# VectorE reads a finished projection step before it splits the next weights, in sixteen steps of a hybrid decoder layer

## The chip, the cores and the metric

The kernel runs on one core of one Trainium2 chip. The metric is the device time of one execution in microseconds (us); several executions of a kernel are compared by their median.

## The reference

One inference step of a one-layer decoder trunk over 320 tokens (256 of a prompt and 8 x 8 new ones), in float32. All token vectors go through one large input projection; two branches are then computed from its parts, merged and projected out. Cut to what matters here:

```python
def layer(x, p, s0, g_pre, w_in, g_v, w_s, b_s, w_a2, b_a, g_o, w_pa, w_pb, w_o, g_post, w_pg, w_pe):
    xn = rms_norm(x, g_pre)
    u_a, v_a, z_a, q_b, k_b, v_b, z_b, a_lr, m_a, m_b = split_cols(xn @ w_in)
    v_a = rms_norm(v_a, g_v)
    y_a = chunk_spatial_gate(u_a, v_a, w_s, b_s) * jax.nn.silu(z_a)
    log_a = jax.nn.log_sigmoid((a_lr @ w_a2 + b_a).astype(jnp.float32)) / GATE_TAU
    ...
    o, s_new = gla(q, k, v, log_a.reshape(B, L, HB, DK), s0)
    y_b = rms_norm(o, g_o).reshape(B, L, E_B) * jax.nn.silu(z_b)
    m = jax.nn.sigmoid(m_a) * (y_a @ w_pa) + jax.nn.sigmoid(m_b) * (y_b @ w_pb)
    h = x + rms_norm(m @ w_o, g_post)
    h = h + jax.nn.sigmoid(h @ w_pg) * (p @ w_pe)
    return h, s_new, v_a
```

The change touches the columns `v_b` (1024 wide: the values of the gated linear attention `gla`) and `z_b` (1024 wide: the gate of its output).

## The kernel before

**Steps and units.** Every projection is cut into steps of 128 output features. A step is a product of 16 blocks of 128 x 128 weights with all 320 tokens and ends up in one PSUM bank; its weights come as two units of 8 blocks (512 KB each). The order of the steps is fixed by the constants S_K, S_Q, S_V, S_ZB, S_VA, S_ZA, S_U, S_GATE and so on: four k steps, four q steps, eight v steps (s = S_V + t), eight z steps (s = S_ZB + t), eight va steps and further ones. In the v and z steps a step's bank is `bank[s % 2]`.

**Split products.** To keep float32 accuracy each unit is split into a rounded part and a rest: ScalarE writes `w_hi` = rounded(`w_raw`) (`split_hi`, L416), VectorE writes `w_lo` = `w_raw` - `w_hi` (`low`, L739, called twice by `split_lo`, and called "a rest" below). TensorE multiplies hi x hi, hi x lo and lo x hi (`product`, L1382 to L1384), 24 matmuls a unit and 48 a step.

**The ring.** `w_raw`, `w_hi` and `w_lo` have four slots, so units run two steps ahead: in step s, ScalarE and VectorE split the units of step s + 2. Half 0 of `split_lo(s)` waits until TensorE has used the first unit of step s, half 1 until it has used the second one, which is the end of step s. SP issues the load of unit u as soon as the rest of unit u - 4 is written (semaphore lo_ready, L377 and L338).

**Who reads a bank.** When step s has ended (`sums(s)` waits for it) VectorE scales the bank by the tokens' norm. In the v steps it writes `v_b` (L948 before); in the z steps `gate_input` (L964) writes `tmp`, which waits in addition for the gate of two steps before. Both count up acc_read. TensorE starts step s only when step s - 2 has been read (same bank). ScalarE's `sigmoid(s)` (L481) waits for the read of step s and stands behind both halves of its `split_hi(s)`; GpSimd's `gate` (L1291) multiplies the two.

**What else VectorE does in these steps.** After read and rests come, in v step 0, `spans` (L815 to L818), then `gla_inputs` (decay products of q and k), and in v step 4 to z step 7 transposes of 32 x 32 blocks that turn v and k into token rows (`v_to_tokens` L934, `k_to_tokens` L970). In z step 0 it masks the attention blocks (L985, L991). The transposes of z step 6 complete `v_tokens`. ScalarE rounds them in z step 7 (`round_v(1)`, L493), GpSimd writes their rests in two instructions (`split_v`, L1299; semaphore vp_lo), and TensorE's eight `o_and_state` products behind z step 7 (L1486 to L1488) need them: product 4 the first of the two, product 6 the second, product 7 also the read of z step 7. In the last step of this stretch:

```python
                if t == 7:
                    pe.wait_ge(ak_split, 6)
                    pe.wait_ge(acc_read, S_VA - 1)
                    for i in range(KE):
                        if i in (0, 4, 6):
                            pe.wait_ge(vp_lo, {0: 1, 4: 2, 6: 3}[i])
                        if i == KE - 1:
                            pe.wait_ge(acc_read, S_VA)
                        o_and_state(i)
```

Every engine works through its instructions in the order in which they are written; nothing else orders them but semaphores.

Of the kernel before, what the change touches and what calls it, by code (L numbers as in the profile page):

```python
# [101 lines left out]
def build(nc, A, O):  # L102
    ctx = ExitStack()
    with ctx:
# [618 lines left out]
        def _(dve):  # L723
# [12 lines left out]
            def low(q, ready, used):  # L736
                dve.wait_ge(hi_ready, ready)
                dve.wait_ge(units_used, used)
                dve.tensor_tensor(wlo[:, q], raw[:, q], whi[:, q].bitcast(F32), ALU.subtract).then_inc(lo_ready, 1)  # L739

            def split_lo(s, i=None, halves=(0, 1)):

                for half in halves:
                    u = 2 * (s + 2) + half
                    low(2 * (s % 2) + half, *((u + 1, u - 3) if i is None else (4 * i + (u + 1), 4 * i + (u - 3))))

            def sums(s, i=None, by=4):

                dve.wait_ge(units_used, 2 * s + 2 if i is None else by * i + (2 * s + 2))
# [58 lines left out]
            def spans():  # L808

                prompt = [x[:, :, 0:SEQ].rearrange("p h (c t) -> p h c t", t=BLK) for x in (cum, q_mid, k_dec)]  # L810
                dec = [x[:, :, SEQ:T].rearrange("p h (c t) -> p h c t", t=DEC_L) for x in (cum, k_dec)]
                mid = prompt[0][:, :, :, MID:MID + 1].to_broadcast([P, HB, NBLK, BLK])
                end = prompt[0][:, :, :, BLK - 1:BLK].to_broadcast([P, HB, NBLK, BLK])
                end_d = dec[0][:, :, :, DEC_L - 1:DEC_L].to_broadcast([P, HB, DEC_B, DEC_L])
                dve.tensor_tensor(prompt[1], prompt[0], mid, ALU.subtract).then_inc(spans_ready, 1)  # L815
                dve.tensor_copy(q_mid[:, :, SEQ:T], cum[:, :, SEQ:T]).then_inc(spans_ready, 1)
                dve.tensor_tensor(prompt[2], end, prompt[0], ALU.subtract).then_inc(spans_ready, 1)
                dve.tensor_tensor(dec[1], end_d, dec[0], ALU.subtract).then_inc(spans_ready, 1)  # L818
# [97 lines left out]
            def k_dec_to_tokens(n):  # L916

                ct, pf = n // 4, n % 4
                rows, to = slice(BLK * ct, BLK * ct + BLK), slice(BLK * pf, BLK * pf + BLK)
                dve.transpose(k_ts[rows, :].rearrange("p (h f) -> p h f", f=DK)[:, :, to],  # L920
                              k_dec[to, :, SEQ + BLK * ct:SEQ + BLK * ct + BLK]).then_inc(kts_ready, 1)

            def v_dec_to_tokens(n):

                ct, pf = n // 4, n % 4
                rows, to = slice(BLK * ct, BLK * ct + BLK), slice(BLK * pf, BLK * pf + BLK)
                dve.transpose(v_ts[rows, :].rearrange("p (i f) -> p i f", f=P)[:, :, to],
                              v_sb[to, :, SEQ + BLK * ct:SEQ + BLK * ct + BLK]).then_inc(vts_ready, 1)
# [9 lines left out]
            def some_v_to_tokens(s):  # L938
                if s in VT_STEPS:
                    first, n = VT_STEPS[s]  # L940
                    dve.wait_ge(acc_read, S_V + 4 if first + n <= 16 else S_V + KE)
                    for m in range(first, first + n):
                        v_to_tokens(m)

            for t, s in enumerate(range(S_V, S_ZB)):
                split_lo(s)
                sums(s)
                acc_t.up(dve.tensor_tensor(v_sb[:, t, :], bank[s % 2][:, 0:T], r, ALU.mult))  # L948
                if t == 0:
                    spans()  # L950
                else:
                    gla_inputs(t - 1)
                if t >= 6:
                    dve.wait_ge(dve_own, own.value)
                    for n in range(4 * (t - 6), 4 * (t - 6) + 4):
                        k_dec_to_tokens(n)
                some_v_to_tokens(s)

            def gate_input(s, n):

                sums(s)
                if n >= 2:
                    dve.wait_ge(gate_ready, n - 1)
                acc_t.up(dve.tensor_tensor(tmp[:, s % 2, :], bank[s % 2][:, 0:T], r, ALU.mult))  # L964

            def k_to_tokens(n):

                ct, pf = n // 4, n % 4
                rows, to = slice(BLK * ct, BLK * ct + BLK), slice(BLK * pf, BLK * pf + BLK)
                dve.transpose(ak[rows, :, :, SEQ:SEQ + DK].rearrange("p c h f -> p h c f")[:, :, :, to],  # L970
                              k_256[to, :, :].rearrange("p h (c q t) -> p h c q t", c=2, t=BLK)[:, :, :, ct, :])\
                   .then_inc(kdt_ready, 1)

            for t, s in enumerate(range(S_ZB, S_VA)):
                split_lo(s)
                gate_input(s, t)
                if t == 0:

                    dve.wait_ge(att_zeroed, 4)
                    dve.wait_ge(att_done, 1)  # L980
                    for c in range(2):
                        for g in range(4):
                            b0, b1 = BLK * g, BLK * g + BLK
                            mask = con[b0:b1, C_ATT + b0:C_ATT + b1].bitcast(I32).unsqueeze(1).to_broadcast([BLK, HB, BLK])
                            last = dve.copy_predicated(ak[b0:b1, c, :, P * c + b0:P * c + b1], mask,  # L985
                                                       bank[4][b0:b1, P * c:P * c + P]
                                                       .rearrange("p (h t) -> p h t", h=HB))
                        last.then_inc(att_masked, 1)
                    for h in range(HB):
                        r0 = DEC * (h % 2)  # L990
                        last = dve.copy_predicated(att_s[:, h, :], con[r0:r0 + DEC, C_ATS:C_ATS + DEC].bitcast(I32),  # L991
                                                   bank[3][r0:r0 + DEC, DEC * (h // 2):DEC * (h // 2) + DEC])
                    last.then_inc(att_masked, 1)
                if t == 1:
                    dve.wait_ge(acc_read, S_V + KE)
                    for n in range(2 * (P // BLK)):
                        v_dec_to_tokens(n)
                some_v_to_tokens(s)
                if s in KT_STEPS:
                    first, n = KT_STEPS[s]  # L1000
                    dve.wait_ge(gla_in, 6)
                    for m in range(first, first + n):
                        k_to_tokens(m)
# [763 lines left out]
```

## Time and profile before

| | us |
|---|---|
| median of 3 executions | 952.49 (952.32 to 952.87) |
| the profiled execution | 952.29 |
| its span, first to last instruction | 950.3 |
| TensorE (PE) busy | 945.9 (100%) |
| VectorE (DVE) busy | 569.3 (60%) |
| ScalarE (ACT) busy | 377.3 (40%) |
| GpSimd (POOL) busy | 122.9 (13%) |

The profile's page gives busy time by engine, the chain of work that ended last, and groups of instructions. The trace behind it gives every instruction with its start and duration. A matmul of 320 columns is shown with 0.31 us, but matmuls are pipelined and start 0.147 us apart (24 of them make 3.52 us, a unit; 48 make 7.04 us, a step), so a short pause of TensorE doesn't show as idle time and has to be read from the distance between starts. The granted TensorE clock is at full speed in all 40 slices of the page. The v steps run from about 66 to 122.4 us, the z steps from there to 181.5 us (with 2.1 us of attention matmuls behind the first), and the `o_and_state` products to 188.6 us.

### The profile page before, as it was taken

How to read it: one execution, taken by the hardware profiler on the slowest of the kernel's cores; microseconds unless marked ns; L12 is line 12 of the kernel's file. 1: busy time of each engine (PE TensorE's matmuls, PEld its weight loads, DVE VectorE, ACT ScalarE, POOL GpSimd, SP SyncE). 2: the span in 40 equal slices, each digit the busy share in tenths (PEclk: the TensorE clock that was granted, in tenths of full speed). 3: DMA queues.
4: the chain of work that ended last, by engine and by line, in shares of the span. 5: the costliest groups of instructions: out<-in, count | busy, mean ns of one | idle time of the engine just before them, and what ended most of it. 6: DMA issues, size and time to landing. Idle time of an engine off the chain costs nothing.

```text
span 950.3 us, 17375 instructions
## 1 busy us (share of the span) xinstructions
PE 945.9 (100%) x6632; PEld 939.0 (99%) x6632; DVE 569.3 (60%) x800; ACT 377.3 (40%) x484; POOL 122.9 (13%) x113
## 2 busy tenths in 40 slices
PE   9999999999999999999999999999999999999998
PEld 9999999999999999999999999999999999999998
DVE  6948779737889866444444444444445444597442
ACT  7545245522353444333333333333333233555331
POOL 1000005504212740000000000000002433100000
PEclk9999999999999999999999999999999999999999
DMA  9545436977654544444444444444447444336541
GB/s 349 181 131 182 142 128 196 229 253 256 221 157 155 186 141 154 154 154 145 144 153 154 135 154 153 154 141 146 154 155 268 145 154 154 111 134 227 176 157 37
DMA packets 56671, 159.69 MB, mean 168 GB/s; under 512 B 6452, under 2 KB 20280, under 8 KB 56632
## 3 DMA queue, kind: packets, MB, share of 16 engines
q1 hardware_dynamic: 42496, 143.05, 45.8%
q10 hardware_dynamic: 14136, 16.10, 5.1%
q8 instruction: 27, 0.44, 0.2%
q14 instruction: 12, 0.10, 0.0%
HBM read 149.94 MB, written 9.18 MB: 167 GB/s over the span
## 4 chain that ended last, share of the span: by engine, by line
PE 100%; DVE 0%; issue 0%; POOL 0%; DVEq 0%; POOLq 0%
PE bank L1382 30%; PE bank L1384 30%; PE bank L1383 30%; PE bank L1443 1%; PE bank L1452 1%; PE bank L1642 1%; PE bank L1636 1%; PE bank L1446 1%; PE bank L1639 1%; PE bank L1415 0%; PE bank L1413 0%; PE bank L1414 0%; PE bank L1420 0%; PE bank L1546 0%; PE bank L1585 0%; PE bank L1486 0%
## 5 line engine op out<-in xcount | busy, mean ns | idle before, releaser
L739 DVE TENSOR_TENSOR w_lo<-w_raw,w_hi 128x1024 fp32r<-128x1024 f32 x252 | 314.4, 1253 | 319.8 <-ACT w_hi L633 165.9
L1382 PE MATMUL bank<-x_hi,w_hi 128*128 128x320 f32 x1216 | 376.6, 310 | 0.0
L1384 PE MATMUL bank<-x_hi,w_lo 128*128 128x320 f32 x1216 | 375.7, 309 | 0.0
L1383 PE MATMUL bank<-x_lo,w_hi 128*128 128x320 f32 x1216 | 375.7, 309 | 0.0
L416 ACT ACTIVATE w_hi<-w_raw 128x1024 fp32r<-128x1024 f32 x148 | 156.0, 1058 | 252.8 <-PE bank L1384 234.9
L1382 PEld LDWEIGHTS bank<-x_hi,w_hi 128*128 128x128 f32 x1216 | 228.2, 188 | 2.0 <-issue 1.8
L1383 PEld LDWEIGHTS bank<-x_lo,w_hi 128*128 128x128 f32 x1216 | 228.2, 188 | 0.0
L1384 PEld LDWEIGHTS bank<-x_hi,w_lo 128*128 128x128 f32 x1216 | 228.2, 188 | 0.0
L633 ACT ACTIVATE w_hi<-w_raw 128x1024 fp32r<-128x1024 f32 x96 | 101.7, 1059 | 115.7 <-PE bank L1384 115.7
L1382 PE MATMUL bank<-m_hi,w_hi 128*128 128x320 f32 x448 | 138.4, 309 | 0.0
L1383 PE MATMUL bank<-m_lo,w_hi 128*128 128x320 f32 x448 | 138.4, 309 | 0.0
L1384 PE MATMUL bank<-m_hi,w_lo 128*128 128x320 f32 x448 | 138.4, 309 | 0.0
L1382 PEld LDWEIGHTS bank<-m_hi,w_hi 128*128 128x128 f32 x448 | 84.1, 188 | 0.0
L1383 PEld LDWEIGHTS bank<-m_lo,w_hi 128*128 128x128 f32 x448 | 84.1, 188 | 0.0
L1384 PEld LDWEIGHTS bank<-m_hi,w_lo 128*128 128x128 f32 x448 | 84.1, 188 | 0.0
L1364 POOL TENSOR_TENSOR sig<-mo 128x320 f32<-128x320 f32 x1 | 1.6, 1632 | 376.0 <-DVE mo L1185 376.0
L1382 PE MATMUL bank<-ya_hi,w_hi 128*128 128x320 f32 x128 | 39.6, 309 | 0.0
L1383 PE MATMUL bank<-ya_lo,w_hi 128*128 128x320 f32 x128 | 39.6, 309 | 0.0
L1384 PE MATMUL bank<-ya_hi,w_lo 128*128 128x320 f32 x128 | 39.6, 309 | 0.0
L1382 PE MATMUL bank<-yb_hi,w_hi 128*128 128x320 f32 x128 | 39.6, 309 | 0.0
L1383 PE MATMUL bank<-yb_lo,w_hi 128*128 128x320 f32 x128 | 39.6, 309 | 0.0
L1384 PE MATMUL bank<-yb_hi,w_lo 128*128 128x320 f32 x128 | 39.6, 309 | 0.0
(250 smaller groups left out, 924.3 us busy)
## 6 DMA issues: line engine op xcount, KB each, us to landing
w_raw<-in_w_units SPq DMA_DIRECT2D x258, 512.0 KB, 3.3
state_dec<-in_s ACTq DMA_DIRECT2D x8, 512.0 KB, 6.4
out_st_dec<-state_dec ACTq DMA_DIRECT2D x8, 512.0 KB, 5.7
h<-in_x_t ACTq DMA_DIRECT2D x4, 640.0 KB, 8.3
out_y<-pe_out ACTq DMA_DIRECT2D x16, 160.0 KB, 2.5
x_sb<-in_x_t SPq DMA_DIRECT2D x6, 320.0 KB, 7.6
v_rows<-v_parts SPq DMA_DIRECT2D x4, 256.0 KB
v_stacked_rows<-v_rows SPq DMA_DIRECT2D x4, 256.0 KB, 6.4
```

The lines of the kernel that those rows point to most:

```text
L416: act.activation(whi[:, q], raw[:, q], ACT.Copy).then_inc(hi_ready, 1)
L633: act.activation(whi[:, q], raw[:, q], ACT.Copy).then_inc(hi_ready, 1)
L739: dve.tensor_tensor(wlo[:, q], raw[:, q], whi[:, q].bitcast(F32), ALU.subtract).then_inc(lo_ready, 1)
L1382: pe.matmul(acc, h, hi[:, k0 + k, :], start=first and k == 0, stop=False)
L1383: pe.matmul(acc, h, lo[:, k0 + k, :], start=False, stop=False)
L1384: m = pe.matmul(acc, l, hi[:, k0 + k, :], start=False, stop=last and k == UK - 1)
L1443: pe.matmul(bank[n][:, 0:T], whi[:, c % 4, w, :], xhi[:, k, :], start=k == 0, stop=False)
L1446: pe.matmul(bank[n][:, 0:T], whi[:, c % 4, w, :], xlo[:, k, :], start=False, stop=False)
L1452: m = pe.matmul(bank[n][:, 0:T], wlo[:, c % 4, w, :], xhi[:, k, :], start=False, stop=k == KX - 1)
L1636: pe.matmul(bank[PG_BANKS[n]][:, 0:T], whi[:, c % 4, w[n], :], mhi[:, k, :], start=k == 0, stop=False)
L1639: pe.matmul(bank[PG_BANKS[n]][:, 0:T], whi[:, c % 4, w[n], :], mlo[:, k, :], start=False, stop=False)
L1642: m = pe.matmul(bank[PG_BANKS[n]][:, 0:T], wlo[:, c % 4, w[n], :], mhi[:, k, :], start=False, stop=k == KX - 1)
```

## The change

In the eight v steps the read of the finished step (`sums(s)` and the product with `r`) now stands ahead of both rests of `split_lo(s)`; in the eight z steps `gate_input(s, t)` stands ahead of them. Nothing is added or removed, and only VectorE's order changes.

```diff
@@ -943,9 +943,9 @@
             for t, s in enumerate(range(S_V, S_ZB)):
-                split_lo(s)
                 sums(s)
                 acc_t.up(dve.tensor_tensor(v_sb[:, t, :], bank[s % 2][:, 0:T], r, ALU.mult))
+                split_lo(s)
                 if t == 0:
                     spans()
                 else:
@@ -972,8 +972,8 @@
             for t, s in enumerate(range(S_ZB, S_VA)):
+                gate_input(s, t)
                 split_lo(s)
-                gate_input(s, t)
                 if t == 0:
```

VectorE at the first two v steps; `v_b` is written by the read, `w_lo` by the rests, `decay_cum` by the last work of the q steps, and q_mid and k_dec by `spans`:

```order
 L857 SCALAR_TENSOR_TENSOR decay_cum<-consts,k_dec 128x320 x4
-L739 TENSOR_TENSOR w_lo<-w_raw,w_hi 128x1024 x2
-L948 TENSOR_TENSOR v_b<-bank,r_tok 128x320
+L947 TENSOR_TENSOR v_b<-bank,r_tok 128x320
+L739 TENSOR_TENSOR w_lo<-w_raw,w_hi 128x1024 x2
 L815 TENSOR_TENSOR q_mid<-decay_cum 128x4x256
 L816 COPY q_mid<-decay_cum 128x4x64
 L817 TENSOR_TENSOR k_dec<-decay_cum 128x4x256
 L818 TENSOR_TENSOR k_dec<-decay_cum 128x4x64
```

The read has moved ahead of two rests; what follows stands where it stood.

VectorE at the fifth to seventh z step (t = 4 to 6); `tmp` is written by the read, `att_and_kd` and `v_tokens` by the transposes:

```order
-L739 TENSOR_TENSOR w_lo<-w_raw,w_hi 128x1024 x2
-L964 TENSOR_TENSOR tmp<-bank,r_tok 128x320
+L964 TENSOR_TENSOR tmp<-bank,r_tok 128x320
+L739 TENSOR_TENSOR w_lo<-w_raw,w_hi 128x1024 x2
 L970 STREAM_TRANSPOSE att_and_kd<-k_67 32x4x2x32 x8
-L739 TENSOR_TENSOR w_lo<-w_raw,w_hi 128x1024 x2
-L964 TENSOR_TENSOR tmp<-bank,r_tok 128x320
+L964 TENSOR_TENSOR tmp<-bank,r_tok 128x320
+L739 TENSOR_TENSOR w_lo<-w_raw,w_hi 128x1024 x2
 L934 STREAM_TRANSPOSE v_tokens<-v_b 32x4x2x32 x8
```

Between the transposes of one step and the rests of the next there now stands a wait for the end of that next step; before, only the second of the two rests waited for it.

## Rows read from the trace of the kernel before

**Rows 1.** page, part 1, whole run: engine, busy us (share of the span) xinstructions
```profile
PE 945.9 (100%) x6632; PEld 939.0 (99%) x6632; DVE 569.3 (60%) x800; ACT 377.3 (40%) x484; POOL 122.9 (13%) x113
```

**Rows 2.** page, part 4, the chain that ended last, share by engine
```profile
PE 100%; DVE 0%; issue 0%; POOL 0%; DVEq 0%; POOLq 0%
```

**Rows 3.** all waits of PE: engine line <- releaser: us, times, longest
```profile
PE bank L1420 <- POOL att_and_kd L1270: 1.1, 1, 1.1
```

**Rows 4.** timeline of PE, 79.7 to 80.4: start us, us, instruction
```profile
79.75 0.31 PE L1384 MATMUL bank<-x_hi,w_lo 128*128 128x320 f32 x1
79.97 0.41 PE L1382 MATMUL bank<-x_hi,w_hi 128*128 128x320 f32 x1
80.21 0.30 PE L1383 MATMUL bank<-x_lo,w_hi 128*128 128x320 f32 x1
80.36 0.31 PE L1384 MATMUL bank<-x_hi,w_lo 128*128 128x320 f32 x1
```

**Rows 5.** timeline of DVE, end of the q steps and first v steps
```profile
77.07 2.36 DVE L739 TENSOR_TENSOR w_lo<-w_raw,w_hi 128x1024 fp32r<-128x1024 f32 x2
79.35 0.48 DVE L948 TENSOR_TENSOR v_b<-bank,r_tok 128x320 f32<-128x320 f32 x1
79.75 1.21 DVE L815 TENSOR_TENSOR q_mid<-decay_cum 128x1024 f32<-128x1024 f32 x1
```

**Rows 6.** timeline of ACT, v steps and z steps six to eight
```profile
94.40 1.06 ACT L416 ACTIVATE w_hi<-w_raw 128x1024 fp32r<-128x1024 f32 x1 [2.45 <-PE bank L1384]
...
104.96 1.06 ACT L416 ACTIVATE w_hi<-w_raw 128x1024 fp32r<-128x1024 f32 x1 [2.46 <-PE bank L1384]
...
167.70 1.06 ACT L416 ACTIVATE w_hi<-w_raw 128x1024 fp32r<-128x1024 f32 x1 [2.46 <-PE bank L1384]
170.45 0.47 ACT L481 ACTIVATE sig<-tmp 128x320 f32<-128x320 f32 x1 [1.69 <-DVE tmp L964]
...
174.74 1.06 ACT L416 ACTIVATE w_hi<-w_raw 128x1024 fp32r<-128x1024 f32 x1 [0.78 <-PE bank L1384]
...
181.88 1.06 ACT L493 ACTIVATE v_tokens_hi<-v_tokens 128x1024 fp32r<-128x1024 f32 x1 [2.33 <-DVE v_tokens L934]
```

**Rows 7.** timeline of DVE, fourth v step and z steps five to eight
```profile
92.26 1.23 DVE L739 TENSOR_TENSOR w_lo<-w_raw,w_hi 128x1024 fp32r<-128x1024 f32 x1
...
163.54 3.72 DVE L970 STREAM_TRANSPOSE att_and_kd<-k 32x256 f32<-32x256 f32 x8
...
174.05 1.40 DVE L739 TENSOR_TENSOR w_lo<-w_raw,w_hi 128x1024 fp32r<-128x1024 f32 x1
175.83 1.86 DVE L739 TENSOR_TENSOR w_lo<-w_raw,w_hi 128x1024 fp32r<-128x1024 f32 x1 [0.39 <-ACT w_hi L416]
...
178.12 3.72 DVE L934 STREAM_TRANSPOSE v_tokens<-v_b 32x256 f32<-32x256 f32 x8
...
183.92 1.48 DVE L739 TENSOR_TENSOR w_lo<-w_raw,w_hi 128x1024 fp32r<-128x1024 f32 x1 [0.82 <-ACT w_hi L416]
```

**Rows 8.** loads of w_raw issued from 73 to 130, us to landing
```profile
DMA to landing us min/median/max: 3.1/3.3/4.8
```

**Rows 9.** the same of all weight loads
```profile
DMA to landing us min/median/max: 3.0/3.3/10.5
```

**Rows 10.** timeline of POOL at the seventh and eighth z step
```profile
174.32 4.66 POOL L1306 TENSOR_TENSOR att_and_kd_lo<-att_and_kd,att_and_kd_hi 128x512 fp32r<-128x512 f32 x3
...
183.02 3.54 POOL L1299 TENSOR_TENSOR v_tokens_lo<-v_tokens,v_tokens_hi 128x512 fp32r<-128x512 f32 x2 [3.20 <-ACT v_tokens_hi L493]
```

**Rows 11.** the first of the two instructions of the last row alone
```profile
183.02 1.29 POOL L1299 TENSOR_TENSOR v_tokens_lo<-v_tokens,v_tokens_hi 128x512 fp32r<-128x512 f32 x1 [3.20 <-ACT v_tokens_hi L493]
```

**Rows 12.** timeline of PE, seventh o_and_state product and its neighbour
```profile
186.71 0.28 PE L1488 MATMUL bank<-att_and_kd_hi,v_tokens_lo 128*128 128x256 f32 x1
186.83 0.34 PE L1486 MATMUL bank<-att_and_kd_hi,v_tokens_hi 128*128 128x384 f32 x1
```

## The prediction

> **What bounds the kernel now.** I read the page's busy times first, then the chain of waits, then TensorE's own waits, and only then the timelines of the sixteen steps. TensorE is busy for 945.9 of 950.3 us [rows 1] and the chain that ended last is TensorE at 100% [rows 2]. In the whole run it has one wait that the trace lists, 1.1 us before its very first matmuls [rows 3], far from the v and z steps. VectorE is busy for 60% [rows 1]. So what VectorE does earlier or later counts only where TensorE waits for it. The question is then not how much earlier the bank is read, but which instruction of TensorE stood behind that read before, and which one stands behind something that is now later.
>
> TensorE's pauses are hidden by pipelined durations, so I looked at distances between starts. In the v and z steps 320-column matmuls start 0.147 us apart (80.21 to 80.36 is 0.15). There is one exception that concerns this change: at the border between v steps 1 and 2 the starts are 79.75, 79.97, 80.21 [rows 4]. Two distances take 0.46 us in place of 2 x 0.147 = 0.29, so 0.17 us are lost. The third v step needs the bank of the first, and VectorE read that bank from 79.35 for 0.48 us, to 79.83 [rows 5]; TensorE goes on 0.14 us later. The read was late because VectorE was late from its work on the decays: it came free at 77.07 and then did two rests, 2.28 us from start to the read's start [rows 5].
>
> **What the change does, part by part.**
>
> The eight v reads. The only one TensorE waited for is the first. It now starts at 77.07, as its step ended a step's length before the pause, at about 72.9, and nothing else holds it, and ends at 77.55, 2.3 us before TensorE asks. That pause goes: minus 0.17 us. The two rests behind it end 0.40 us later (79.35 less 0.08 of overlap in place of 79.75 is where the next work begins [rows 5]), at about 78.7 and 79.8. TensorE needs the first at 79.9, so 1.2 us of cover remain, and the second 3.5 us later. `spans` starts where it did, at 79.75, since the same three instructions stand ahead of it. What would be late next is the first rest; it would have to lose 1.2 us.
>
> The other reads, seven v and eight z. A read may be as late as the end of the following step, 7.04 us after its own, so moving it from 2.3 us behind the end to the end itself brings nothing: 0 us.
>
> What follows the rests. The decay products of v step 7, which TensorE needs 7.04 us after that step's end, and the masks of z step 0 start at most 0.5 us later (2.7 us behind the end where it was 2.3; in z step 0 VectorE waits for 2.1 us of attention matmuls anyway). Nothing that TensorE waits for within a step hangs on them. Cost 0 us.
>
> The rests. In a v step without a backlog the first rest ran in mid-step: in v step 3 from 92.26 to 93.49 [rows 7], where the step ended when ScalarE began its second half at 94.40 [rows 6]. Now it must wait for that end and the read: 94.40 + 0.40 + 1.23 = 96.0, 2.5 us later. TensorE uses it at the end of the next step, 101.4; 5.4 us of cover. The second rest waited for ScalarE (1.06 us) and ran to 94.40 + 2.3; now to 94.40 + 0.40 + 2.4 = 97.2, against a use at 104.9. Cost 0 us.
>
> The loads behind the rests. SP issues a load when a rest is written, so one of two loads is also up to 2.5 us later. The one that follows the rest of v step 3 would go out at 96.0. The longest landing between 73 and 130 us is 4.8 us [rows 8], so 100.8, and ScalarE rounds this unit at 104.96 [rows 6]: 4.1 us of cover. With the longest landing of the whole run, 10.5 us [rows 9], it would be 106.5. ScalarE would be 1.6 us late, but VectorE asks for the result only at 108.5 + 0.4, and TensorE at 115.5. In the z steps VectorE was already late for its first rest (its transposes ended at 163.54 + 3.72 = 167.26, the step at 167.70 [rows 6, 7]), so loads move by only 1 us there. Cost 0 us.
>
> The sigmoid and the gate. `sigmoid` waited for the read: in z step 5 it ran at 170.45, though ScalarE was free at 167.70 + 1.06 = 168.76 [rows 6]. It now goes at once, and GpSimd's gate and what follows it come up to 1.7 us earlier. No product waits for a gate here, but this moves GpSimd's long instructions against VectorE's rests, which matters next.
>
> The transposes and what hangs on them. After the step's end there came, before, 1.09 us of waiting for ScalarE, one rest and the read: the transposes of z step 4 began at 163.54, 2.9 us after the end at 160.66 (167.70 less a step). Now come the read and two rests: 0.40 + 2.28 = 2.7 us, more if the rests are stretched. In z step 6 the distance was 178.12 - 174.74 = 3.38 us, as the rests took 1.40 and 1.86 us while GpSimd worked from 174.32 on, in place of 1.23 [rows 6, 7, 10]. The new distance lies between 2.7 us (no rest is stretched) and 2.7 + 2 x 0.63 + 0.15 = 4.1 us (both like the worse one), that is from 0.7 earlier to 0.7 later. Since GpSimd's block moves ahead by up to 1.7 us, I take 0.3 us earlier.
>
> From here a chain with very little cover leads to TensorE. The transposes end at 181.84; ScalarE rounds from 181.88 [rows 6]; GpSimd writes two rests from 183.02 to 186.56 [rows 10], the first 1.29 us [rows 11], the second 2.24, stretched by 0.95, while VectorE's rest ran from 183.92, itself 1.48 us instead of 1.23 [rows 7]. The seventh product starts at 186.83 [rows 12], 0.27 us after GpSimd's end; 0.14 us of this is what a released TensorE needed above. The true cover is 0.13 us, and since TensorE comes 0.17 us earlier, it is due by 186.66. The new order: transposes end about 181.5, GpSimd starts at about 182.7, takes again 3.54 us, and ends at 186.2, with 0.3 us to spare. But VectorE's two rests now lie at about 182.0 and 183.7, so both can meet GpSimd's two instructions. Bounds: no stall, if the pair meets one rest as before, and 0.7 + 0.95 - 0.13 + 0.17 = 1.7 us, if the transposes are late by the full 0.7 and the first instruction is stretched as the second was. I take 0, as the nearest row is this pair with one meeting.
>
> The rows show the collision as a stretch: 1.86 for 1.23, 2.24 for 1.29. The Trainium skill, on its page "SBUF — State Buffer", section "Who interferes with whom", has a harsher rule: a VectorE instruction with two SBUF inputs contends with a GpSimd instruction that reads SBUF through a port held exclusively, so that the one that comes second is blocked until the other has ended. By this rule the two engines would take turns at z step 7, which is rival B.
>
> Sum in the profiled execution's own time: 952.29 - 0.17 + 0 = 952.12 us. The three runs shown have a median of 952.49, 0.2 us above the profiled one, so I forecast 952.3 us as a median. That is 0.02% less, and this kernel's measurement can't tell less than about 0.2% (1.9 us) from no change.
>
> **Rivals.**
>
> B. VectorE and GpSimd take turns. Place: the pair of GpSimd rests ahead of product 6. GpSimd wants to begin at 182.7, waits for VectorE's rest until 183.2, ends at 184.5; VectorE's second rest waits for that and ends at 185.7; GpSimd's second instruction only then runs, to 187.0. With 0.14 us TensorE goes on at 187.1, not at 186.66: a stall of about 0.5 us, net plus 0.3, thus 952.8. The bound of 1.7 us gives 954.0. It decides from the point where the pair takes more than 3.9 us in place of 3.54. For it: this is the only place in the two stages where TensorE's cover is a tenth of a microsecond. Against it: GpSimd's earlier block leaves VectorE freer in z step 6, so the chain may start earlier.
>
> C. The later loads starve the ring. Place: w_raw's slots in the v and z steps. It decides when a load takes more than 115.5 - 96.0 - 1.06 - 1.23 = 17 us. Price: each microsecond above this is a microsecond of TensorE in each of up to sixteen steps, so one more in all would be 968. Against it: the longest of all landings is 10.5 us [rows 9].
>
> D. A gain above 0.2%. It needs 1.9 us of TensorE's pauses in the two stages. For it: the read frees a bank 2.3 us earlier in most steps. Against it: the starts show 0.17 us of pause that this can remove. Time 950.4, if there were pauses that the records hide.
>
> E. The change does not do what it says, because VectorE arrives late at most steps. In the z steps it was free only 0.4 us ahead of the step's end (167.26 against 167.70), so stretched instructions could push the read back behind the end again. Time as in the forecast or, if also the first v read is still late, 952.5.
>
> **Chances.** Forecast, hidden but for the 0.17 us: 0.70, with its own range of 952.0 to 952.8 (the spread of the runs shown is 0.55 us). B: 0.23. C: 0.02. D: 0.02. E: 0.03. Together, range 951.9 to 953.4: it takes in all of the forecast and E and most of B. Faster by over 0.2%: 0.02 (D). Slower by over 0.2%: 0.03, from C and the far end of B. Within 0.2%: 0.95.
>
> **What would show it.** The starts around 79.9 us are 0.15 apart, with the v read of step 0 near 77.1. The z reads start within 0.2 us of ScalarE's second half, and the sigmoids directly behind it. The rests in v steps lie as a pair behind the read. The list of TensorE's waits stays as short as it is. For B, a distance between starts well above 0.18 us ahead of the seventh `o_and_state` product, and a pair of L1299 that takes over 3.9 us. I am wrong if the time leaves 952.3 by more than 1.9 us, or if TensorE pauses at any other border of the two stages.

## The result: slower by 0.36%, outside the forecast range

| | kernel before | changed kernel |
|---|---|---|
| median, us (7 runs each) | 952.53 (951.91 to 952.92) | 956.35 (954.53 to 956.51) |
| the profiled execution, us | 952.29 | 955.05 |
| its span, us | 950.3 | 953.2 |

The ratio is 1.0036, with a 95% interval of 1.0026 to 1.0046. The forecast was 952.3 us, with a range of 951.9 to 953.4.

The seven runs of the changed kernel form two groups: 954.53 and 955.05 us with a mean granted clock of 1.000, and five from 956.33 to 956.51 us with 0.998 (the granted clock is the share of TensorE's full speed that the chip let it run at, here as the mean of a run). The profiled execution, 955.05 us, is of the first group. So there are two things to explain: 2.9 us of span, and 1.3 to 1.5 us on top of that in most runs.

The page of the changed kernel, parts 1 and 4, answers to [rows 1, 2]:

```profile
PE 946.4 (99%) x6632; PEld 939.4 (99%) x6632; DVE 572.5 (60%) x800; ACT 377.3 (40%) x484; POOL 126.2 (13%) x113
...
PE 96%; DVE 3%; issue 1%; POOL 0%; ACT 0%; DVEq 0%; POOLq 0%
```

TensorE's work is the same, but it no longer makes up the whole chain; VectorE holds 3% of it. All waits of TensorE, to be held against [rows 3]:

```profile
PE bank L1486 <- POOL v_tokens_lo L1299: 2.4, 2, 2.2
PE bank L1420 <- POOL att_and_kd L1270: 1.1, 1, 1.1
```

There is a new wait, 2.4 us in two pieces, for GpSimd's rests of `v_tokens`. The timeline of TensorE there (with the products counted from 0, 184.91 is the last matmul of product 3, 187.38 the first of product 4, 189.61 the first of product 6):

```profile
184.91 0.28 PE L1488 MATMUL bank<-att_and_kd_hi,v_tokens_lo 128*128 128x256 f32 x1
187.38 0.44 PE L1486 MATMUL bank<-att_and_kd_hi,v_tokens_hi 128*128 128x384 f32 x1 [2.19 <-POOL v_tokens_lo L1299]
187.66 0.34 PE L1487 MATMUL bank<-att_and_kd_lo,v_tokens_hi 128*128 128x384 f32 x1
...
189.14 0.28 PE L1488 MATMUL bank<-att_and_kd_hi,v_tokens_lo 128*128 128x256 f32 x1
189.61 0.45 PE L1486 MATMUL bank<-att_and_kd_hi,v_tokens_hi 128*128 128x384 f32 x1 [0.19 <-POOL v_tokens_lo L1299]
```

Neighbouring starts are 0.12 us apart at such places. 187.38 - 184.91 - 0.12 is 2.35 us, 189.61 - 189.14 - 0.12 is 0.35 us, and the first matmul behind each pause is followed after 0.28 to 0.29 us where 0.18 is usual. Together 2.9 us, the whole difference of the spans. (Product 6 stood at 186.83 before [rows 12].) The next step then begins at 191.49 in place of 188.60, and nothing behind it gives anything back.

Where GpSimd got late is seen by going back: ScalarE's rounding (L493), then GpSimd's pair of rests.

```profile
184.58 1.06 ACT L493 ACTIVATE v_tokens_hi<-v_tokens 128x1024 fp32r<-128x1024 f32 x1 [5.20 <-DVE v_tokens L934]
```

In [rows 6] ScalarE began this at 181.88. It is 2.7 us late because VectorE's transposes ended 2.7 us late. The timeline of VectorE from z step 3 to z step 6 (L964 is the read, L739 the two rests, L970 and L934 the transposes):

```profile
153.54 0.49 DVE L964 TENSOR_TENSOR tmp<-bank,r_tok 128x320 f32<-128x320 f32 x1 [0.53 <-PE bank L1384]
153.94 5.52 DVE L739 TENSOR_TENSOR w_lo<-w_raw,w_hi 128x1024 fp32r<-128x1024 f32 x2
159.39 3.69 DVE L970 STREAM_TRANSPOSE att_and_kd<-k 32x256 f32<-32x256 f32 x8
163.11 0.49 DVE L964 TENSOR_TENSOR tmp<-bank,r_tok 128x320 f32<-128x320 f32 x1
163.51 3.04 DVE L739 TENSOR_TENSOR w_lo<-w_raw,w_hi 128x1024 fp32r<-128x1024 f32 x2
...
170.34 0.49 DVE L964 TENSOR_TENSOR tmp<-bank,r_tok 128x320 f32<-128x320 f32 x1
170.75 3.04 DVE L739 TENSOR_TENSOR w_lo<-w_raw,w_hi 128x1024 fp32r<-128x1024 f32 x2
...
177.43 0.49 DVE L964 TENSOR_TENSOR tmp<-bank,r_tok 128x320 f32<-128x320 f32 x1
177.84 2.96 DVE L739 TENSOR_TENSOR w_lo<-w_raw,w_hi 128x1024 fp32r<-128x1024 f32 x2
180.82 3.72 DVE L934 STREAM_TRANSPOSE v_tokens<-v_b 32x256 f32<-32x256 f32 x8
```

The read of z step 3 is on time, then its pair of rests takes 5.52 us. Alone two rests take 2.35. The first of the two by itself:

```profile
153.94 3.28 DVE L739 TENSOR_TENSOR w_lo<-w_raw,w_hi 128x1024 fp32r<-128x1024 f32 x1
```

And GpSimd over the same time:

```profile
149.96 3.81 POOL L1306 TENSOR_TENSOR att_and_kd_lo<-att_and_kd,att_and_kd_hi 128x1024 fp32r<-128x1024 f32 x3
153.73 2.41 POOL L1322 TENSOR_TENSOR v_parts<-v_tokens_dec,v_parts 64x1024 fp32r<-64x1024 f32 x1
156.10 2.28 POOL L1322 TENSOR_TENSOR k_parts<-k_tokens_dec,k_parts 64x512 fp32r<-64x512 f32 x1
...
164.18 1.29 POOL L1291 TENSOR_TENSOR zb_gate<-tmp,sig 128x320 f32<-128x320 f32 x1 [3.98 <-ACT sig L481]
...
185.72 3.84 POOL L1299 TENSOR_TENSOR v_tokens_lo<-v_tokens,v_tokens_hi 128x512 fp32r<-128x512 f32 x2 [4.18 <-ACT v_tokens_hi L493]
```

GpSimd began the 2.41 us instruction that reads v_tokens_dec (L1322) at 153.73, 0.21 us ahead of VectorE's rest. The rest takes 3.28 us and ends 1.08 us behind the end of GpSimd's instruction, which is about its own length. GpSimd's next one (1.28 us when alone) then takes 2.28. They did not share time, they took turns. In the kernel before, the same place looked like this on GpSimd:

```profile
150.72 5.88 POOL L1306 TENSOR_TENSOR att_and_kd_lo<-att_and_kd,att_and_kd_hi 128x1024 fp32r<-128x1024 f32 x3
156.56 2.40 POOL L1322 TENSOR_TENSOR v_parts<-v_tokens_dec,v_parts 64x1024 fp32r<-64x1024 f32 x1
```

There v_parts ran from 156.56, when VectorE was at its transposes, which do not slow it (2.40 us).

From z step 4 on the lag of 2.5 us is not worked off. From read to read VectorE needs 7.23, 7.09 and 7.15 us (163.11, 170.34, 177.43, 184.58), and TensorE 7.04. The late pairs of rests take 2.96 to 3.04 us, since a GpSimd instruction gets in between the two: in z steps 4 and 5 it is the gate, at 164.18 and 171.41, in z step 6 the last part of the split of the attention block (L1306), which began at 177.98 and took 1.73 us.

### The profile page after: what moved, and what is told of

Same layout as the page of the kernel before. It is cut to its first block, busy times and chain, and to the rows that moved or that the text cites. A ratio compares the mean times of both kernels' runs of the same rounds, so it can differ in the third digit from the quotient of the medians.

```text
span 953.2 us, 17379 instructions
## 1 busy us (share of the span) xinstructions
PE 946.4 (99%) x6632; PEld 939.4 (99%) x6632; DVE 572.5 (60%) x800; ACT 377.3 (40%) x484; POOL 126.2 (13%) x113
## 4 chain that ended last, share of the span: by engine, by line
PE 96%; DVE 3%; issue 1%; POOL 0%; ACT 0%; DVEq 0%; POOLq 0%
PE bank L1382 29%; PE bank L1384 29%; PE bank L1383 29%; DVE w_lo L739 2%; PE bank L1443 1%; PE bank L1636 1%; PE bank L1452 1%; PE bank L1446 1%; PE bank L1642 1%; PE bank L1639 1%; PE bank L1414 0%; PE bank L1415 0%; PE bank L1413 0%; DVE v_tokens L934 0%; DVE att_and_kd L970 0%
## 5 line engine op out<-in xcount | busy, mean ns | idle before, releaser
L739 DVE TENSOR_TENSOR w_lo<-w_raw,w_hi 128x1024 fp32r<-128x1024 f32 x252 | 317.6, 1270 | 303.2 <-ACT w_hi L633 165.9
```

## The experiments

All were timed beside the kernel before (27 runs of it in each of two batches, medians 952.55 and 952.49 us).

**V steps alone.**

```diff
             for t, s in enumerate(range(S_V, S_ZB)):
-                split_lo(s)
                 sums(s)
                 acc_t.up(dve.tensor_tensor(v_sb[:, t, :], bank[s % 2][:, 0:T], r, ALU.mult))
+                split_lo(s)
```

> The kernel before with the new order in the eight v steps alone; the z steps keep the old one. Theory 1 (all of the loss comes from the z steps, where VectorE's rests meet GpSimd's instructions; GpSimd does nothing in the v steps): 952.3 us, the pause of 0.17 us at 79.9 us gone, rests in z step 3 at 1.2 to 1.3 us each, no wait of TensorE for v_tokens_lo. Theory 2 (the later rests and loads of the v steps carry a part of the loss): over 953.3 us.

Measured 951.99 us, ratio 0.9996 (0.9987 to 1.0005); no wait of TensorE but the one before its first matmuls; the pause near 79.9 us is gone, and the rests of z step 3 take 1.23 and 1.28 us. The loss is not in the v steps. This is also the lowest median of all kernels here, but it can't be told from no change.

**Z steps alone.**

```diff
             for t, s in enumerate(range(S_ZB, S_VA)):
-                split_lo(s)
                 gate_input(s, t)
+                split_lo(s)
```

> The kernel before with the new order in the eight z steps alone. Theory 1: the whole loss, 956.5 us as a median, a first rest of z step 3 of about 3.3 us and a wait of TensorE of some 2.2 us ahead of the fifth o_and_state product; the runs fall into two groups, near 955 with a granted clock of 1.000 and near 956.5 with 0.998, as those of the changed kernel. Theory 2: clearly less than that, under 955.5.

Measured 956.52 us, ratio 1.0039 (1.0026 to 1.0053), the pair of rests in z step 3 again 5.52 us, and TensorE's longest wait 2.2 us. Two runs lie at 955.28 and 955.41 us (clock 1.000), three from 956.52 to 956.83 (0.998). The z steps carry the whole loss.

**The changed kernel with the old order in z step 3, and the kernel before with the new order in z step 3 alone.**

```diff
             for t, s in enumerate(range(S_ZB, S_VA)):
+                if t == 3:
+                    split_lo(s)
                 gate_input(s, t)
-                split_lo(s)
+                if t != 3:
+                    split_lo(s)
```

(and the reverse: `t != 3` ahead, `t == 3` behind.)

> The changed kernel with the old order in z step 3 alone. There a rest of 3.28 us had begun 0.2 us behind a GpSimd instruction that reads v_tokens_dec. Theory 1a (this one meeting makes the lag, the later steps only keep it): no rest over 1.9 us in z step 3, the transposes of z step 6 start within 0.5 us of 178.1, TensorE stalls 0 to 0.6 us at the o_and_state products, 952.3 to 953.0 us. Theory 1b (each z step loses by the gate that GpSimd now runs during the rests, 3.0 us for the pair in place of 2.3, so the lag builds up anyway): transposes of z step 6 over 1.5 us late, 954.5 us or more.

> The kernel before with the new order in z step 3 alone. GpSimd's split of the attention block starts only at 150.7 us as before, since the sigmoid of z step 2 is not earlier, so the meeting of z step 3 may fall on another of its instructions. Theory 1a: the pair of rests in z step 3 takes 2.4 to 4.5 us; a lag of up to 2 us is worked off by 0.6 us a step in the three steps behind it, as the old order meets no gate in the rests; 952.5 to 953.5 us. Theory 1b: the same place alone costs nothing: 952.5 us.

Old order in z step 3: 954.32 us, ratio 1.0018 (1.0009 to 1.0027). Theory 1a failed in its numbers: going back to the old order there did not keep the rests free. Nor did theory 1b get a clean hit: the transposes of z step 6 started at 179.72, 1.6 us late, and the pairs of rests of z steps 4 and 5 took 3.0 us, as it said, but the time stayed below its 954.5. This run doesn't decide between the two. VectorE, two rests and the read:

```profile
152.87 5.13 DVE L739 TENSOR_TENSOR w_lo<-w_raw,w_hi 128x1024 fp32r<-128x1024 f32 x2
157.92 0.47 DVE L964 TENSOR_TENSOR tmp<-bank,r_tok 128x320 f32<-128x320 f32 x1
```

GpSimd's first reading instruction of L1322 (L1325 in this kernel):

```profile
153.53 3.38 POOL L1325 TENSOR_TENSOR v_parts<-v_tokens_dec,v_parts 64x1024 fp32r<-64x1024 f32 x1
```

The sigmoids and gates of the steps ahead were still early, so v_parts started near 153.5 instead of 156.6. This time VectorE's first rest was there ahead of v_parts (152.87; it took 1.79 us itself, as the last part of GpSimd's L1309 had begun 0.03 us before it), GpSimd waited for it (3.38 us in place of 2.41), and VectorE's second rest waited for GpSimd.

New order in z step 3 alone: 953.79 us, ratio 1.0015 (1.0006 to 1.0024). Theory 1b (952.5 us) falls; theory 1a was right in kind but its bounds were too small, 4.5 us for the pair and 953.5 us for the time. VectorE, read and rests of z step 3, and the transposes of z step 6:

```profile
153.95 0.49 DVE L964 TENSOR_TENSOR tmp<-bank,r_tok 128x320 f32<-128x320 f32 x1 [0.51 <-PE bank L1387]
154.35 5.00 DVE L739 TENSOR_TENSOR w_lo<-w_raw,w_hi 128x1024 fp32r<-128x1024 f32 x2
...
180.01 0.90 DVE L934 STREAM_TRANSPOSE v_tokens<-v_b 32x256 f32<-32x256 f32 x2
```

GpSimd (L1309 and L1325 are L1306 and L1322 of the kernel before):

```profile
151.11 3.81 POOL L1309 TENSOR_TENSOR att_and_kd_lo<-att_and_kd,att_and_kd_hi 128x1024 fp32r<-128x1024 f32 x3
154.89 3.39 POOL L1325 TENSOR_TENSOR v_parts<-v_tokens_dec,v_parts 64x1024 fp32r<-64x1024 f32 x1
```

Here nothing of GpSimd's was early. But the wait for the step's end leaves VectorE idle from about 153.4 to 153.95; GpSimd's two short instructions of the attention split are no longer held up by rests (3.81 us for the three, 5.88 before), and v_parts comes at 154.89, behind the start of the pair, which takes 5.0 us. So both parts of the new order lead to the same meeting: the earlier sigmoid and the later first rest. The lag shrinks behind it, as no gate runs between the rests of z steps 4 and 5 (2.36 us a pair): the transposes of z step 6 start at 180.01, 1.6 us later than in the kernel with the v steps alone.

**GpSimd writes the parts, but reads nothing for them.**

```diff
                     for n, (parts, x) in enumerate(((v_parts, v_ts), (k_parts, k_ts))):
                         pool.wait_ge(parts_hi, n + 1)
-                        pool.tensor_tensor(parts[:, 1, :], x[:], parts[:, 0, :].bitcast(F32), ALU.subtract)\
-                            .then_inc(parts_lo, 1)
+                        pool.memset(parts[:, 1, :].bitcast(F32), 0.0).then_inc(parts_lo, 1)
```

> The changed kernel, but GpSimd fills the rests of v_parts and k_parts (L1322) with zeros and reads nothing for them; so the lower parts of the new tokens' v and k are left out of the computation. Theory 1a, corrected by the two runs on z step 3 (the rests of z step 3 are held up by whatever long reading instruction GpSimd has under way, and the lag is kept since each later pair of rests meets a gate): the pair of rests in z step 3 takes 2.3 to 3.0 us, the transposes of z step 6 start at about 178.1 instead of 180.8, TensorE stalls under 0.6 us, 952.3 to 953.0 us. Rival 3 (the instructions compete in some other way, by their number or their writes): the pair still takes over 4 us and the time stays over 954.5.

Measured 952.73 us, ratio 1.0001 (0.9992 to 1.0010). The pair of rests in z step 3 on VectorE, and the two fills on GpSimd at the same moment:

```profile
154.19 2.35 DVE L739 TENSOR_TENSOR w_lo<-w_raw,w_hi 128x1024 fp32r<-128x1024 f32 x2
```

```profile
153.95 0.95 POOL L1322 MEMSET v_parts<- 64x1024 f32 x1
154.84 0.52 POOL L1322 MEMSET k_parts<- 64x512 f32 x1
```

With fills of 0.95 and 0.52 us right beside it the pair takes 2.35 us, its length alone. The loss is gone. The transposes of z step 6 start at 178.48, and TensorE waits for nothing there. (The fills are also shorter than the instructions that they replace, so the time alone would not tell reading from length. But the first fill runs from 153.95 to 154.90, and the first rest, which starts at 154.19, isn't stretched. Whether a fill is longer beside a rest than alone was not measured.)

**The same work one gate later.**

```diff
                 if t == 2:
                     split_att_and_kd(0, 0, SEQ)
+                if t == 3:
                     for n, (parts, x) in enumerate(((v_parts, v_ts), (k_parts, k_ts))):
```

> The changed kernel, but GpSimd's two long instructions L1322 stand one gate later, so that they fall beside VectorE's transposes of z step 3 and not beside its rests. Theory 1a: 952.3 to 953.0 us with the new order kept everywhere, the pair of rests in z step 3 under 3.3 us. Rival 4 (any order with the read first loses in the z steps, as rest and gate collide each time): the transposes of z step 6 still over 1.5 us late and over 954 us.

Measured 952.49 us, ratio 1.0000 (0.9991 to 1.0009), with the new order in all sixteen steps and nothing left out. VectorE in z steps 3 and 6:

```profile
153.62 0.49 DVE L964 TENSOR_TENSOR tmp<-bank,r_tok 128x320 f32<-128x320 f32 x1 [0.53 <-PE bank L1385]
154.03 2.35 DVE L739 TENSOR_TENSOR w_lo<-w_raw,w_hi 128x1024 fp32r<-128x1024 f32 x2
...
174.74 0.49 DVE L964 TENSOR_TENSOR tmp<-bank,r_tok 128x320 f32<-128x320 f32 x1 [0.68 <-PE bank L1385]
175.15 3.14 DVE L739 TENSOR_TENSOR w_lo<-w_raw,w_hi 128x1024 fp32r<-128x1024 f32 x2
178.33 1.84 DVE L934 STREAM_TRANSPOSE v_tokens<-v_b 32x256 f32<-32x256 f32 x4
```

GpSimd in z step 3 (the gate, then v_parts):

```profile
155.18 1.94 POOL L1291 TENSOR_TENSOR zb_gate<-tmp,sig 128x320 f32<-128x320 f32 x1 [1.34 <-ACT sig L481]
157.08 2.40 POOL L1323 TENSOR_TENSOR v_parts<-v_tokens_dec,v_parts 64x1024 fp32r<-64x1024 f32 x1
```

v_parts now runs beside the transposes in 2.40 us. The gate takes 1.94 us in place of 0.88, as it waits for the second rest, but the rests keep their 2.35. Rival 4 falls: reading first costs nothing in the z steps as long as no lag puts the gate ahead of a rest. That order is close: the second rest starts at 155.16, 0.02 us ahead of the gate, which is why a lag that brings the sigmoid directly behind the read turns it round.

**The sigmoid as late as before.**

```diff
                 split_hi(s, halves=(1,))
+                act.wait_ge(lo_ready, 2 * (s + 2) + 2)
                 sigmoid(s)
```

> The changed kernel, but in the z steps ScalarE's sigmoid waits until both rests of its step are written, so the gate runs beside the transposes as before. Theory 5 (the earlier sigmoid and gate are the cause: they bring GpSimd's long instructions forward): no meeting in z step 3, 952.3 to 952.8 us. Theory 1a: the pair of rests in z step 3 still takes 4.5 to 5.5 us, as with the new order in that step alone, then the lag shrinks by about 0.6 us a step; time between that of z step 3 alone and that of the changed kernel, 953.8 to 954.8 us, and no gate over 0.9 us.

Measured 954.14 us, ratio 1.0017 (1.0008 to 1.0026). v_parts takes 3.38 us from 154.66, all gates 0.87 or 0.88 us, and TensorE waits 1.4 us in two pieces. Theory 5 falls as the only cause: with GpSimd's start as before, the meeting still takes place. All numbers of theory 1a were met: the pair of rests in z step 3 takes 4.96 us, those of z steps 4 and 5 take 2.35, and the lag shrinks by 0.5 to 0.7 us a step. What the early gates add is that the lag is kept. In the profiled executions, both at the full clock, this is 0.8 us of span (952.4 to 953.2); the rest of the rise of the medians, from 954.1 to 956.4 us, goes with the lower clock of most runs of the changed kernel, which the next run takes up.

**A pause of TensorE by itself**, in the kernel before.

```diff
                 if t == 7:
+                    for _ in range(16):
+                        then(pool.memset(zb_gate[:, 7, :], 0.0))
                     split_v(4, 2)
```

> The kernel before, with 16 needless fills of an unused row block on GpSimd in z step 7 ahead of its two rests of v_tokens, so that TensorE waits 2.5 to 4.5 us ahead of the fifth o_and_state product and nothing else changes. Theory 6 (a pause of TensorE of about 2.5 us or more costs some 1.5 us beyond its own length in most runs, seen as a granted clock of 0.998, which is why the changed kernel's median is 3.8 us up and its profiled run only 2.5): the median is the pause plus 1.5 to 2 us over the kernel before, runs in the upper group show a clock of 0.998. Rival: the median is up by the length of the pause alone and the clock stays 1.000.

The one wait that it adds to TensorE's:

```profile
PE bank L1488 <- POOL v_tokens_lo L1299: 2.7, 1, 2.7
```

Measured 956.36 us, ratio 1.0040 (1.0026 to 1.0054): 955.51 and 955.56 us at a clock of 1.000, and 956.36, 956.48 and 956.68 at 0.998. By the starts the pause is 2.84 us (188.17 - 185.21 - 0.12). A pause with next to nothing else changed gives both groups, so the rival falls and theory 6 stands in kind. Its size was too high: the lower group is 3.0 us over the kernel before, the pause and 0.1 us behind it, and the upper group lies 0.8 to 1.2 us above the lower one, not 1.5 to 2. In the changed kernel and with the z steps alone the groups are 1.1 to 2.0 us apart; why more was not found out. The three kernels with shorter pauses (1.4 us of listed waits or less: the two on z step 3 and the late sigmoid) have 33 runs, none at 0.998. How the clock's level and these 0.8 to 2.0 us hang together was not shown beyond their coming together, and where the clock falls was not seen, since every profiled execution of the three slowest kernels has 1.000.

## Why the prediction was wrong

- **The read of v step 0: right.** TensorE's starts near 79.9 us, to be held against [rows 4], and VectorE's first v steps against [rows 5]:

```profile
79.75 0.31 PE L1383 MATMUL bank<-x_lo,w_hi 128*128 128x320 f32 x1
79.90 0.31 PE L1384 MATMUL bank<-x_hi,w_lo 128*128 128x320 f32 x1
80.05 0.31 PE L1382 MATMUL bank<-x_hi,w_hi 128*128 128x320 f32 x1
```

```profile
77.22 0.49 DVE L947 TENSOR_TENSOR v_b<-bank,r_tok 128x320 f32<-128x320 f32 x1
77.63 2.35 DVE L739 TENSOR_TENSOR w_lo<-w_raw,w_hi 128x1024 fp32r<-128x1024 f32 x2
79.90 1.22 DVE L815 TENSOR_TENSOR q_mid<-decay_cum 128x1024 f32<-128x1024 f32 x1
...
94.40 0.49 DVE L947 TENSOR_TENSOR v_b<-bank,r_tok 128x320 f32<-128x320 f32 x1 [2.21 <-PE bank L1384]
94.80 2.35 DVE L739 TENSOR_TENSOR w_lo<-w_raw,w_hi 128x1024 fp32r<-128x1024 f32 x2
```

The 0.17 us pause is gone, the read starts where VectorE came free (77.22; this execution is 0.14 us later from its start on), `spans` follows at 79.90. In v step 3 the read starts at the step's end and the pair behind it takes 2.35 us, as worked out. The time alone can't confirm 0.17 us; the trace does.

- **Reads, and loads behind the rests: right.** No read was waited for, and no load. The longest landing of a weight load, against [rows 9]:

```profile
DMA to landing us min/median/max: 3.0/3.3/10.6
```

- **The transposes and what hangs on them: this step failed.** The prediction set the distance from the end of z step 6 to its transposes between 2.7 and 4.1 us. It was 180.82 - 174.72 = 6.1. Three things in it were wrong. First, the stretch of a rest was bounded by the worst one that the old trace showed, 1.86 us, that is by 0.63. The right bound was the length of the longest reading instruction of GpSimd that can stand ahead of a rest, 2.40 us (v_parts at 156.56 in the kernel before, shown above); measured were 3.28 - 1.23 = 2.05. The old rows already told of turns and not of a mild stretch: the rest of 1.48 us at 183.92 [rows 7] ended at 185.40, 1.09 us behind the end of GpSimd's first instruction (183.02 + 1.29 [rows 11]), and GpSimd's second one ended 1.16 us behind that rest. Each took about its own length once the other had ended; the stretch was small only because little of the other one was left. Second, only z steps 6 and 7 were searched for meetings, as the chain to TensorE starts there. The meeting came in z step 3, where GpSimd's v_parts had missed VectorE's rests before and now met them. Third, nothing was said of a lag that is kept. Read, two rests and transposes need 6.4 us of the 7.04 if nothing disturbs them, but 7.1 to 7.2 with a GpSimd instruction between the rests.

- **The small cover at product 6: right that it decides, slightly wrong in size.** The 0.14 us that were taken off the 0.27 us had been measured behind a VectorE instruction. Behind GpSimd's L1299 TensorE started after 0.05 us (in the changed kernel from 187.33 to 187.38, in the kernel with the pause from 188.12 to 188.17), so the cover was about 0.22 us and not 0.13. What went beyond it arrived at TensorE: 2.7 us of lag and 0.3 us by which GpSimd's pair got longer (3.84 against 3.54), less the cover, are the 2.8 us by which product 6 started late (189.61 against 186.83), and the slower second start behind the pause adds 0.1.

- **"GpSimd's block moves ahead ..., I take 0.3 us earlier": wrong in sign.** That the sigmoid and the gate come earlier was right (sigmoid at 154.56 behind the read of z step 3). It was counted as relief, and it was one part of the cause; the transposes of z step 6 came 2.7 us later.

- **Rival B had the engines, the mechanism and the last link, but the wrong place and size.** It let the engines take turns in z step 7 and priced this at 0.5 us, 1.7 at most. The Trainium skill's rule, on its page "SBUF — State Buffer", section "Who interferes with whom", was put there alone. By this rule, applied in z step 3, a rest that comes 0.21 us behind a 2.41 us instruction of GpSimd would wait an estimated 2.2 us; the trace agrees with its 2.05, and the fills that read nothing agree with it too, as the same section exempts GpSimd instructions that only write.

- **The median's last 1.3 us** were in no rival. A pause of TensorE was priced at its own length; the run with a pause by itself shows 0.8 to 1.2 us more in three of five runs, at the lower clock.

- C and D did not occur. E did in part: the reads of z steps 4 to 7 came 2.5 to 2.8 us behind the end, as a result of the lag and not as its cause.

## What to carry to other kernels

When an order is changed on an engine that shares something with another one, lay both engines' timelines of the whole stretch side by side and look for the long instruction that just misses the moved one. Bound a meeting by the length of the other engine's instruction, not by the worst stretch seen so far, and then ask whether the lag can be worked off before someone with little cover asks for the result. Where the new order is wanted, it is often enough to move the other engine's long instruction to a moment when no one competes with it.

## What the runs showed of the hardware

- A VectorE instruction with two SBUF inputs and a GpSimd instruction that reads SBUF took turns whole: 1.23 us became 3.28, 1.28 became 2.28, 0.88 became 1.94, and the one that came second waited, even if it came only 0.2 us behind (v_parts at 153.73, the rest at 153.94). VectorE's transposes did not disturb GpSimd's reading instructions (2.40 us beside them) and took 3.68 to 3.72 us for eight either way. GpSimd's fills did not disturb VectorE's rests (2.35 us for two).
- TensorE went on 0.05 us behind the end of the GpSimd instruction that released it, and its first matmul behind a pause was followed after 0.28 us where 0.18 is usual.
- With a pause of TensorE of 2.3 to 2.8 us in one piece (the changed kernel, the z steps alone, and the pause by itself) 6 of 17 runs were 2.0 to 3.1 us over the kernel before, and the other 11 were 3.8 to 4.3 us over it, with a mean granted clock of 0.998. In the profiled executions of these three kernels the clock is 1.000.
